# Small steps moved ahead of tile splits, and a reciprocal in two halves

## What is computed

```python
# first block
proj = rmsnorm(x, mix_norm_w) @ w_in              # 36 weight tiles
g    = -exp(a_log) * softplus(a_logit + dt_bias)  # 8 heads x 512 tokens
gc   = cumsum(g)                                  # the decay sums, per chunk
beta = sigmoid(beta_logit)
qkv  = silu(causal_dwconv(qkv, conv_w))           # 4 taps, 24 tiles
# second block
dt   = softplus(dt + dt_bias); a_cs = cumsum(dt * a)
y    = gated_group_rmsnorm(y, z, ssd_norm, 2)     # rsqrt of the mean square of each of 2 groups
```

## Time and profile before

| | us |
|---|---|
| median of 3 runs | 3094.21 |
| lowest and highest run | 3093.58, 3099.11 |
| the profiled execution | 3101.02 |
| its span, first to last instruction | 3099.1 |
| PE busy | 2961.9 (96%) |
| DVE busy | 2120.1 (68%) |
| ACT busy | 1286.4 (42%) |
| mean granted clock of PE | 0.979 |

### The profile page before, as it was taken

One profiled execution on the slowest core, in us unless ns is written; L12 is line 12 of the kernel. 1 busy time (PEld: TensorE's weight loads), 2 busy tenths in 40 slices (PEclk: granted clock), 3 DMA queues, 4 the chain that ended last, 5 costly groups with the idle time before them and its releaser, 6 DMA issues. The chain is left out here.

```text
span 3099.1 us, 42070 instructions
## 1 busy us (share of the span) xinstructions
PE 2961.9 (96%) x14292; PEld 2403.6 (78%) x14292; DVE 2120.1 (68%) x3975; ACT 1286.4 (42%) x1949; POOL 491.9 (16%) x532
## 2 busy tenths in 40 slices
PE   7999999998989889999999999999998999999998
PEld 5678876887877777788888888888886867766787
DVE  5574434346888958798888988888895584446334
ACT  4443343333367752344444444444444343434222
POOL 1013442002467630000000000000001031024000
PEclk8999999999999999999999999999999999999999
DMA  2220001332234354433343344443342211200322
GB/s 107 75 68 23 27 25 69 115 116 89 85 120 170 140 218 133 139 128 120 126 135 123 120 135 135 135 135 118 120 141 77 95 49 62 85 24 1 123 95 89
DMA packets 138193, 316.99 MB, mean 102 GB/s; under 512 B 9296, under 2 KB 74960, under 8 KB 135888
## 3 DMA queue, kind: packets, MB, share of 16 engines
q1 hardware_dynamic: 133376, 280.33, 27.7%
q10 hardware_dynamic: 4688, 34.98, 2.8%
HBM read 275.43 MB, written 39.85 MB: 102 GB/s over the span
## 5 line engine op out<-in xcount | busy, mean ns | idle before, releaser
L205 DVE TENSOR_TENSOR split<-raw,split 128x1024 fp32r<-128x1024 f32 x172 | 209.8, 1226 | 411.3 <-ACT split L196 402.4
L196 ACT ACTIVATE split<-raw 128x1024 fp32r<-128x1024 f32 x216 | 227.0, 1057 | 598.3 <-PE proj L222 165.1
L2281 PE MATMUL up<-up_high,weight_high 128*128 128x512 f32 x700 | 272.3, 389 | 0.0
L2282 PE MATMUL up<-up_low,weight_high 128*128 128x512 f32 x700 | 272.3, 389 | 0.0
L2283 PE MATMUL up<-up_high,weight_low 128*128 128x512 f32 x700 | 272.3, 389 | 0.0
L373 POOL TENSOR_TENSOR xl<-col,xh 128x512 fp32r<-128x512 f32 x8 | 10.0, 1269 | 1073.6 <-ACT xh L345 1073.6
L1815 PEld LDWEIGHTS score<-hot,hot 128*128 128x128 f32 x1024 | 132.3, 197 | 44.7 <-DVE hot L2007 20.3
L1815 PE MATMUL score<-hot,hot 128*128 128x128 f32 x1024 | 139.1, 283 | 26.9 <-DVE hot L2007 12.1
L2410 PE MATMUL dt<-xh,split 128*128 128x512 f32 x416 | 162.0, 389 | 2.4 <-ACTq L2528 1.8
L2411 PE MATMUL dt<-xl,split 128*128 128x512 f32 x416 | 161.9, 389 | 0.0
L2412 PE MATMUL dt<-xh,split 128*128 128x512 f32 x416 | 161.8, 389 | 0.0
(11 more groups left out here) (547 smaller groups left out, 7821.6 us busy)
## 6 DMA issues: line engine op xcount, KB each, us to landing
raw<-in_stream SPq DMA_DIRECT2D x440, 512.0 KB, 3.5
gates<-stage ACTq DMA_DIRECT2D x16, 2048.0 KB, 6.5
gate<-gates SPq DMA_DIRECT2D x31, 1024.0 KB, 8.0
h<-in_x SPq DMA_DIRECT2D x4, 512.0 KB, 6.0
h<-in_x SPq DMA_DIRECT2D x1, 2048.0 KB, 8.7
h_saved<-h SPq DMA_DIRECT2D x1, 2048.0 KB, 7.5
h<-h_saved SPq DMA_DIRECT2D x1, 2048.0 KB, 14.7
rows<-h SPq DMA_DIRECT2D x4, 512.0 KB, 2.6
```

The source lines that it names most:

```text
L196: act.activation(g.high[t % slots], g.raw[:, t % RAW, :], ACT.Copy).then_inc(g.high_split, 1)
L205: dve.tensor_tensor(g.low[t % slots], g.raw[:, t % RAW, :], g.high[t % slots], ALU.subtract).then_inc(g.low_split, 1)
L2281: pe.matmul(bank, wh, uh, start=start, stop=False, skip_group_check=True)
L2282: pe.matmul(bank, wh, ul, start=False, stop=False, skip_group_check=True)
```

## The change

Four moves. In `opening` the high halves of tiles 0 and 1 are made behind the loop, and the low halves ahead of the last `columns`. In `delta_front` the softplus chain stands ahead of the high half of tile 2, with `v` and the cleared rows ahead of the low half. In `delta_front` and `project_ssd` the two copies stand ahead of the low half of tile 6. In `project_attention` the mean and the reciprocal of a group follow its own sum, at steps 4 and 8, with the semaphore counts of `root` raised by one.

```diff
@@ opening
-                    if t >= 2:
-                        split_high(g, act, 0, t - 2)
+                for j in range(2):
+                    split_high(g, act, 0, j)
                 norm.split_columns(act, TT - 1)
...
-                norm.columns(dve, TT - 1, weight)
                 for j in range(2):
                     split_low(g, dve, 0, j)
+                norm.columns(dve, TT - 1, weight)
@@ delta_front, ACT
                 for j in range(N_CONV):
-                    split_high(g, act, 0, j + 2)
-                    if j == 0:
+                    if j:
+                        split_high(g, act, 0, j + 2)
+                    else:
                         act.activation(neg_a[0:8, :], g.heads[0:8, 0:1], ACT.Exp).then_inc(rate_made, 1)
...
                         act.activation(rows[32:40, :], rows_ps[32:40, :], ACT.Sigmoid).then_inc(soft, 1)
+                        split_high(g, act, 0, 2)
                         act.wait_ge(cleared, 1)
@@ delta_front, DVE (the removed lines stood behind split_low, at j == 0 and j == 4)
+                    if j == 0:
+                        dve.tensor_scalar(v[0:8, :], rows_ps[0:8, :], g.heads[0:8, 1:2], None, ALU.add).then_inc(soft, 1)
+                        dve.memset(rows[:, :], 0.0).then_inc(rows_cleared, 1)
+                    if j == 4:
+                        dve.wait_ge(turned, TT)
+                        cols = cols_ps[:, :].rearrange("p (c n) -> p n c", n=P)
+                        dve.tensor_copy(sum_c[:, :, :], cols[:, 0:8, :]).then_inc(tail, 1)
+                        dve.tensor_copy(beta_c[:, :, :], cols[:, 32:40, :]).then_inc(tail, 1)
                     split_low(g, dve, 0, j + 2)
@@ project_ssd, DVE (they stood behind split_low)
+                    if p == 4:
+                        dve.wait_ge(turned, TT)
+                        cols = cols_ps[:, :].rearrange("p (c n) -> p n c", n=P)
+                        dve.tensor_copy(g.sum_c[:, :, :], cols[:, 0:nh, :]).then_inc(tail, 1)
+                        dve.tensor_copy(g.dt_c[:, :, :], cols[:, 32:32 + nh, :]).then_inc(tail, 1)
                     split_low(g, dve, 0, p + 2)
@@ project_attention, DVE
                     split_low(g, dve, 0, j + 2)
-                    if j == DC:
-                        for q in range(SSD_GROUPS):
-                            dve.wait_ge(summed, per * (q + 1))
-                            dve.tensor_scalar(v[:, q, :], means[q], 1.0 / (per * P), EPS, ALU.mult,
-                                              ALU.add).then_inc(root, 1)
-                        dve.wait_ge(root, 2)
-                        dve.reciprocal(t[:, :, :], v[:, :, :]).then_inc(root, 1)
+                    if j in (per, 2 * per):
+                        q = j // per - 1
+                        dve.wait_ge(summed, j)
+                        dve.tensor_scalar(v[:, q, :], means[q], 1.0 / (per * P), EPS, ALU.mult,
+                                          ALU.add).then_inc(root, 1)
+                        dve.wait_ge(root, 2 * q + 1)
+                        dve.reciprocal(t[:, q, :], v[:, q, :]).then_inc(root, 1)
```

More of the change, by code:

```diff
@@ L1119, in _ @@
                         dve.reciprocal(t[64:, :], v[64:, :]).then_inc(root, 1)
+                    if j == 0:
[6 more added lines that the diff above has]
+                        dve.tensor_copy(beta_c[:, :, :], cols[:, 32:40, :]).then_inc(tail, 1)
                     split_low(g, dve, 0, j + 2)
-                    if j == 0:
-                        dve.memset(rows[:, :], 0.0).then_inc(rows_cleared, 1)
-                        dve.tensor_scalar(v[0:8, :], rows_ps[0:8, :], g.heads[0:8, 1:2], None, ALU.add).then_inc(soft, 1)
                     if j == 1:
@@ L1136, in _ @@
                                                    op0=ALU.mult, op1=ALU.add).then_inc(soft, 1)
[L1137 to L1141, removed]
                     if j == 7:
@@ L2931, in _ @@
                                                    initial=0.0, op0=ALU.mult, op1=ALU.add).then_inc(soft, 1)
[L2932 to L2936, removed]
                     if p == 6:
@@ L3371, in _ @@
                     if j == FIRST_Q + 1:
-                        pe.wait_ge(root, 2)
+                        pe.wait_ge(root, 3)
                         pe.wait_ge(read, FIRST_Q + 1)
@@ L3399, in _ @@
                     if j == ROOT:
-                        act.wait_ge(root, 3)
+                        act.wait_ge(root, 4)
                         act.activation(r[:, :, :], t[:, :, :], ACT.Sqrt).then_inc(root, 1)
@@ L3441, in _ @@
                     split_low(g, dve, 0, j + 2)
-                    if j == DC:
-                        for q in range(SSD_GROUPS):
-                            dve.wait_ge(summed, per * (q + 1))
-                            dve.tensor_scalar(v[:, q, :], means[q], 1.0 / (per * P), EPS, ALU.mult,
-                                              ALU.add).then_inc(root, 1)
-                        dve.wait_ge(root, 2)
-                        dve.reciprocal(t[:, :, :], v[:, :, :]).then_inc(root, 1)
+                    if j in (per, 2 * per):
[5 more added lines that the diff above has]
+                        dve.reciprocal(t[:, q, :], v[:, q, :]).then_inc(root, 1)
                     if j == SCALE - 1:
-                        dve.wait_ge(root, 4)
-                        done = refine_root(dve, r[:, :, :], v[:, :, :], t[:, :, :], root, 4)
+                        dve.wait_ge(root, 5)
+                        done = refine_root(dve, r[:, :, :], v[:, :, :], t[:, :, :], root, 5)
                         dve.wait_ge(root, done)
```

## The result

| | before | changed |
|---|---|---|
| median of 8 runs, us | 3098.3 | 3074.53 |
| lowest and highest | 3093.58, 3102.5 | 3070.58, 3087.43 |
| profiled execution, us | 3101.02 | 3074.13 |
| its span | 3099.1 | 3072.2 |

What follows compares the result with a forecast made beforehand. TensorE, busy 96% of the span, was taken as the bound. Gains 2.6 + 1.3 + 10.0 + 4.65 + 4.3 = 22.85 us gave 3078.2 from the profiled 3101.02; the middle of 3071.4 and 3078.2 gave 3074.8, range 3066 to 3083.

Steps and rivals of the forecast that it cites:

- Part A: `opening`: moved low and high halves let `delta_front` start 2.6 us earlier, plus 1.3 of clock in its first tile.
- The clock's 1.3: `delta_front` tile 0: a shorter pause ahead should let it run at 2.4 GHz, winning 1.3 us, bounds 0 and 1.7.
- The upper bound of 1.7: `delta_front` tile 0: most the clock could win, from 7.17 us for that tile against 5.44 steady.
- Part B: `delta_front`: earlier softplus chain wins 4.2 us over tiles 1 to 3, earlier copies 5.8 in tile 5; 10.0 together.
- Part C: `project_ssd`: copies ahead of the low half take 4.65 us off tile 5, from 10.39.
- Part D: `project_attention`: reciprocal in halves lets Sqrt start earlier, winning 4.3 us of the 4.43 lost in tiles 10 and 11.
- the 0.15 at its end: `project_attention`: TensorE can go on at 2655.05 but is free at 2654.90, so the Sqrt chain is late by 0.15 us.
- The sum: Whole kernel: 22.85 us won in the profiled execution, 3078.2; against the shown median, between 3071.4 and 3078.2, middle 3074.8.
- Clock stays: Whole kernel, rival: pauses go but granted clock is lost elsewhere, only 13.1 us won, 3081.1; 8 in 100.
- The wait moves: `project_attention` or `delta_front`, rival: ScalarE becomes late, 3 to 5 us remain there, 3079; 10 in 100.
- No effect: Stages after the changed places, rival: held at a fixed time, they take the gain back, 3094; 3 in 100.
- Slower, by a clock that stays low over whole tiles: First tiles of a stage, rival: low clock adds 5.4 us a tile, six tiles giving 3103; 2 in 100.

Runs made afterwards that it cites:

- evict_first: Kernel before, with only tile 9's eviction put ahead of the root in `project_attention`, reciprocal still whole; tiles 10 and 11 took 11.96 us instead of 15.31.
- made pauses: Changed kernel with four pauses made on purpose in `project_ssd`, lengths rising in one run and falling in another; 3098.5 and 3098.04 us.
- two_more_moves: Changed kernel plus tile 9's eviction ahead of the root in `project_attention` and the softplus chain moved earlier in `project_ssd`; ratio to kernel before 0.9926.
- every part alone: Kernel before with one move at a time; ratios: opening 0.9986, softplus chain 0.9988, both pairs of copies 0.9964, halved reciprocal 0.9990.

## Why the prediction was right, point by point

**Part A.** Start of `delta_front` 31.1 to 31.2 forecast, 31.23 measured; 2.6 against 2.5. The clock's 1.3 was 1.4. The reason given for it was weak, though. The prediction took the pause of 2.18 with a clock of 1.00 as a sign that such a pause is safe. It was one draw: at the same place the clock fell in nine of the twelve traces, behind 2.12 to 2.28, as in the changed kernel and in evict_first (2359.71 to 2367.14, 7.43), at 1.6 a time. What holds is that 1.25 to 1.36 costs nothing, in nine cases of nine (two made pauses, and the start of `delta_front` in seven traces). The upper bound of 1.7 compared two measures: 7.17 was counted from the first matmul, 5.44 from one tile's end to the next. From its first matmul a tile without a pause takes 5.69, so 1.5 was the most.

**Part B.** 4.2 for the tiles up to 3, measured 27.67 - 22.10 less the 1.4 of part A: 4.2. 5.8 for tile 5, measured 5.96. The softplus chain was given at most 7.6; it takes 6.5 (31.20 to 37.73) and makes tile 2's high half 0.7 late at most, under a cover that stands. VectorE's low half for tile 4 starts at 50.00, 3.3 us before tile 3 ends. One reading was off: the copies were said to wait for nothing but transposes done 5.4 us earlier. They also stand behind VectorE's convolution of tile 3 (56.15 to 58.48), so they had 1.7 to spare and not 5.4.

**Part C.** 4.65 forecast, 4.70 measured.

**Part D.** 4.3 forecast, 4.0 measured. The chain was right to 0.1: load, Sqrt, load, eviction, 2637.57 for the matmul. The mis-sized term is the 0.15 at its end. It was reckoned from the end of TensorE's last matmul, which is modelled and lies 0.16 behind the next start at full pace. From start to start it is 2637.03 to 2637.57, 0.54 where 0.23 is the pace: 0.31 lost, and some 0.1 at the restart. two_more_moves, without that chain, gets exactly this 0.43 back.

**The sum.** 22.85 forecast in the profiled execution's own measure, 22.7 measured at the places. The step from there to the median was to take off half of the 6.8 by which the profiled execution was the longer one, on the ground that the clock's share is not in every execution. The table above bears out the ground. The mean cost over its executions is 4.3 (tiles 1 to 3: 20.49 to 20.82 in five traces, against 16.3), 12.23 - 6.80 = 5.4, 9.74 - 5.69 = 4.05 and 14.49 - 11.31 = 3.2, with 3.9 for part A: 20.9, against the 20.4 of the ratio. The size of the step was a guess, and the start it was taken from moved: with more runs the median of before is 3098.3, not 3094.21. 3098.3 - 20.9 = 3077.4 would have been the reasoned figure; that 3074.8 lay nearer to the measured 3074.53 was luck.

**The rivals.** *Clock stays*: rejected by the tile times of every part alone, and by the total: the pauses come to 13.1, the interval begins at 16. *The wait moves*: in D by 0.4, not by 3 to 5; in B not at all. *No effect*: 22.7 at the places, and the ratio keeps 20 of it. That the stages behind take nothing back is known only to within what their own clock does. *Slower, by a clock that stays low over whole tiles*: not at the changed places, and behind the longest made pause, 4.83, it cost at most 2.3. But the prediction saw less of it in one trace than there is: behind the 3.25 at the end of `project_ssd` the clock was 0.50 for ten us or more in seven traces of twelve, which the trace of the kernel before does not show. The Trainium skill's drain of 1.38 us behind each table load (ScalarE: Activation LUTs, "What ACT_TABLE_LOAD costs") shows nowhere in the changed kernel either: in `project_attention` the load at 2633.16 and Sqrt at 2634.45 lie 1.29 apart, load included, and the three-load chain in `delta_front` takes 6.5 us in all.

## What to carry to other kernels

Where two engines feed a third through queues in program order, look at what stands ahead of the instruction that the third waits for: if it waits itself for the third's latest work (a low half behind the end of tile 4), the pause is built in, and putting the small step first costs nothing as long as its input is an older one. Count such a pause with the clock behind it: 0 to 1.6 us on top of 2.5 at most places, up to 3.0 at one; nothing on top of 1.3. And before sizing a change from one trace, ask which of its numbers would be the same in the next execution; the pauses were, to 0.01 us, the clock behind them was not.

## What the runs showed of the hardware

- How often a pause of TensorE was followed by the low clock, over the traces of all twelve kernels:

| pause, us | place | low clock behind it |
|---|---|---|
| 1.25 to 1.36 | start of `delta_front`, two made pauses | 0 of 9 |
| 2.12 to 2.28 | start of `project_ssd` | 9 of 12 |
| 2.44 | two made pauses | 1 of 2 |
| 2.54 | tile 11 of `project_attention` | 2 of 4 |
| 2.56 | tile 3 of `delta_front` | 5 of 5 |
| 2.61 to 2.63 | start of `project_attention` | 12 of 12 |
| 2.73 | behind tile 4 of `delta_front` | 5 of 5 |
| 2.80 | behind tile 4 of `project_ssd` | 3 of 5 |
| 3.25 | start of the stage behind `project_ssd` | 9 of 12 |
| 3.60 to 4.83 | start of `delta_front`, four made pauses | 9 of 9 |

- Where it came within a stage's tiles it cost 1.3 to 1.6 us a time, 1.5 to 3.0 behind the 2.73, and up to 2.3 behind a 4.83; the other 4.83 cost 1.5, as much as a 2.44.
- VectorE's reciprocal takes 3.35 us for 128x512 and 6.55 for 128x1024, five times VectorE's subtraction of 128x1024 (1.23); a half takes half.
- A pause costs about 0.3 us beyond its printed length even at the full clock: tile 5 of `project_ssd` takes 8.78 with a pause of 2.80 and 5.69 without one, and the tile with the made pause of 1.25 takes 7.00 (2477.12 to 2484.12), where 5.44 is the steady distance. 0.16 of it is the modelled end of the last matmul (0.39 long, where the next start is 0.23 away), some 0.1 the distance to the second matmul.
